# First loads in another order in a Conformer and neighbourhood-attention block, with per-tile normalisation and attention blocks taken in pairs

## What is computed

```python
h = _rmsnorm(x, norm_g)                       # x * rsqrt(mean(x*x) + 1e-6) * norm_g
proj = h @ w_in                               # 1024 x 9216
a_val, a_glu, z_a, q, k, v, z_b, g_logits = split(proj)
y_a = (_conv_module(a_val, a_glu, ...) * silu(z_a)) @ w_pw_a      # 31 taps per channel
attn = _neighbourhood_attention(q, k, v, rpb)                     # 16 heads of 64
y_b = (attn * silu(z_b)) @ w_o_b
merged = sigmoid(g_a) * y_a + sigmoid(g_b) * y_b
out = _rmsnorm(x + merged @ w_out, final_g)
```

## Time and profile before

| | us |
|---|---|
| median of three runs (lowest, highest) | 1900.12 (1898.42, 1902.84) |
| the profiled execution: its time, its span | 1902.6, 1900.6 |
| PE busy in the span | 1829.4 (96%) |
| DVE busy | 1101.3 (58%) |
| ACT busy | 541.0 (28%) |
| POOL busy | 202.7 (11%) |

### The profile page before, as it was taken

One profiled execution on the slowest core, in us unless ns is written; L12 is line 12 of the kernel. 1 busy time (PEld: TensorE's weight loads), 2 busy tenths in 40 slices (PEclk: granted clock), 3 DMA queues, 4 the chain that ended last, 5 costly groups with the idle time before them and its releaser, 6 DMA issues.

```text
span 1900.6 us, 25315 instructions
## 1 busy us (share of the span) xinstructions
PE 1829.4 (96%) x9164; PEld 1466.7 (77%) x9164; DVE 1101.3 (58%) x1574; ACT 541.0 (28%) x1105; POOL 202.7 (11%) x241
## 2 busy tenths in 40 slices
PE   4999999999999999999999999999999999999997
PEld 3778877877777787787778778778777777887775
DVE  3210396677477478567747747856874666435133
ACT  4311123223223323322322332332344234103121
POOL 0020001011001101101100110110110054000001
PEclk9999999999999999999999999999999999999998
DMA  6061201312312221221231223123116655442223
GB/s 241 34 122 56 80 23 50 104 37 71 92 40 67 73 76 59 78 84 35 78 90 35 73 67 85 51 78 84 34 56 245 231 177 172 155 133 82 85 101 121
DMA packets 161486, 173.50 MB, mean 91 GB/s; under 512 B 11031, under 2 KB 117543, under 8 KB 161228
## 3 DMA queue, kind: packets, MB, share of 16 engines
q1 hardware_dynamic: 135164, 108.45, 19.2%
q10 hardware_dynamic: 22320, 49.56, 6.8%
q0 software_dynamic: 3872, 13.75, 2.9%
HBM read 121.03 MB, written 50.68 MB: 90 GB/s over the span
## 4 chain that ended last, share of the span: by engine, by line
PE 83%; DVE 7%; DMA 5%; ACT 2%; issue 1%; SPq 0%; POOL 0%; ACTq 0%; DVEq 0%
PE pg L1267 62%; PE pg L1283 9%; PE pO L1382 4%; PE pS L1356 3%; PE pT L1366 3%; DVE work L989 1%; DMA qk<-gb_d 1%; DVE work L1170 1%; DMA y_sample<-work 1%; DMA work<-tb_d 1%; DVE xs L927 1%; DVE ws L918 1%; DMA work<-in_b_gate 1%; ACT ws L584 1%; DMA y_prompt<-work 1%
## 5 line engine op out<-in xcount | busy, mean ns | idle before, releaser
L1267 PE MATMUL pg<-xs,ws 128*128 128x512 f32 x5760 | 1371.9, 395 | 6.4 <-DVE work L1187 6.3
L1267 PEld LDWEIGHTS pg<-xs,ws 128*128 128x128 f32 x5760 | 1069.3, 189 | 247.6 <-issue 23.2
L989 DVE SCALAR_TENSOR_TENSOR work<-work 128x1551 f32<-128x1551 f32 x240 | 439.1, 1830 | 3.5
L1283 PE MATMUL pg<-ws,xs 128*128 128x512 f32 x1152 | 273.0, 398 | 13.7 <-DVE ws L918 9.9
L1283 PEld LDWEIGHTS pg<-ws,xs 128*128 128x128 f32 x1152 | 220.6, 193 | 63.2 <-DVE ws L918 13.0
L918 DVE TENSOR_TENSOR ws<-raw,ws 128x1024 fp32r<-128x1024 f32 x96 | 117.1, 1222 | 162.5 <-ACT ws L584 162.1
L1063 DVE CUSTOM_DVE_ANT_0 work<-pS,work 128x384 f32<-128x384 f32 (+1 forms) x192 | 91.2, 510 | 201.6 <-PE pS L1356 201.5
L778 ACT ACTIVATE work<-work,small 128x384 f32<-128x384 f32 (+1 forms) x192 | 109.9, 574 | 289.3 <-DVE small L1063 289.3
L532 POOL TENSOR_TENSOR work<-work 128x384 f32<-128x384 bf16 (+1 forms) x72 | 61.7, 858 | 1091.0 <-DVE small L1063 1079.7
L584 ACT ACTIVATE ws<-raw 128x1024 fp32r<-128x1024 f32 x96 | 100.9, 1054 | 114.2 <-PE pg L1267 83.2
L1073 DVE TENSOR_SCALAR work<-work,small 128x384 f32<-128x384 f32 (+1 forms) x192 | 111.0, 578 | 6.7
(11 more groups left out here) (88 smaller groups left out, 881.0 us busy)
## 6 DMA issues: line engine op xcount, KB each, us to landing
raw<-in_w_in SPq DMA_DIRECT2D x72, 512.0 KB, 4.0
work<-v_d SPq DMA_DIRECT2D x128, 96.0 KB, 2.8
v_d<-work ACTq DMA_DIRECT2D x24, 256.0 KB, 2.0
za_d<-work ACTq DMA_DIRECT2D x24, 256.0 KB, 2.0
ga_d<-work ACTq DMA_DIRECT2D x24, 256.0 KB, 2.0
gb_d<-work ACTq DMA_DIRECT2D x24, 256.0 KB, 2.0
work<-c_d POOLq DMA_DIRECT2D x8, 768.0 KB, 12.8
qk<-gb_d SPq DMA_DIRECT2D x24, 256.0 KB, 4.0
```

The costliest lines, as they stand in the source:

```text
L989: nc.vector.scalar_tensor_tensor(cv[:, 0:CLEN], u[:, k:k + CLEN], cur[:, k:k + 1], cv[:, 0:CLEN], ALU.mult, ALU.add).then_inc(tap_ok, 1)
L1267: last = nc.tensor.matmul(pg[b][:], ws[:, wslot(s), wpart, k * P:(k + 1) * P], xs[:, k, xpart, chunk(n)], start=(k == 0 and wpart == 1), s ...
L1283: last = nc.tensor.matmul(pg[b][:], xs[:, k, xpart, t * P:(t + 1) * P], ws[:, wslot(s0 + k // 2), wpart, chunk(k % 2)], start=(k == 0 and ...
```

## The change

1. **Loads.** SP issues token tile 0, then the norm weight broadcast to all 128 partitions (`ngb`, 128 rows), weight pieces 0 and 1, token tile 1, pieces 2 and 3, tiles 2 to 7, pieces 4 and 5, tiles 8 to 11, the masks, and only then the parameter rows. Pieces 2 and 3 land in buffers of their own (`raw2`), and piece 4 is split into a spare place (`spare`, in the tile qk), so that pieces 0 to 5 wait less for one another. The relative-position load for the second head of unit 0 stands behind the values' load.
2. **Normalisation by tile.** Squares, mean, power, scaling, transposes and evacuation go tile by tile instead of four tiles at a time; the scaling also multiplies by `ngb`. The eight transposes of tile t+1 stand in the middle of group t. The parameter rows are transposed between the first and the second half.
3. **Attention in pairs.** Blocks 2c and 2c+1 go together: values of the pair before, then scores of both blocks, in four banks pS. The transposes are issued one head at a time, in four places half a slot apart, all in one bank pT. One bank pO is left.

```diff
+X_SLOT = 4
...
-    if S_PRO <= s < S_YB:
-        return s % 2
-    return s % 4 if s < S_PRO else (s + 2) % 4
+    if s < S_PRO + 1:
+        return (0, 1, 2, 3, X_SLOT, 0, 1, 2, 3)[s]
+    return s % 2 if s < S_YB else (s + 2) % 4
...
-        pS = [ctx.enter_context(nc.psum_tensor(f"pS{i}", [P, CH], F32)) for i in range(2)]
-        pT = [ctx.enter_context(nc.psum_tensor(f"pT{i}", [P, CH], F32)) for i in range(2)]
-        pO = [ctx.enter_context(nc.psum_tensor(f"pO{i}", [P, CH], F32)) for i in range(2)]
-        pH = [pT[0], pT[1], pO[0], pO[1]]
+        pS = [ctx.enter_context(nc.psum_tensor(f"pS{i}", [P, CH], F32)) for i in range(4)]
+        pT = ctx.enter_context(nc.psum_tensor("pT", [P, CH], F32))
+        pO = ctx.enter_context(nc.psum_tensor("pO", [P, CH], F32))
+        pH = [pT, pO, pS[2], pS[3]]
...
+        def pair_at(i, slot):
+            c, r = divmod(slot - 1, 2 * spacing(i))
+            return c if r == 0 and 0 <= c <= BLOCKS // 2 else None
+        def transposed_at(i, slot, half):
+            m = 4 * spacing(i)
+            c, r = divmod(2 * slot + half - 2, m)
+            t = r - (6 if spacing(i) == 3 else 4)
+            if 0 <= t < 4 and 0 <= c < BLOCKS // 2:
+                return 2 * c + t // 2, t % 2
+            return None
...
             load_x(0)
-            sp.dma_start(prow[0:TAPS, :], dw_w[0]).then_inc(par_in, 16)
-            for r, src in ((I_DWB, dw_b[0:1, :]), (I_LNG, ln_g[0:1, :]), (I_LNB, ln_b[0:1, :]),
...
+            sp.dma_start(ngb, norm_g[0:1, :].to_broadcast([P, D])).then_inc(ng_in, 16)
             for s in range(2):
                 piece_s(s, w_rows(w0, C_V * P, s))
             load_x(1)
             for s in range(2, 4):
                 piece_s(s, w_rows(w0, C_V * P, s))
-            sp.wait_ge(ht_ps, KT)
-            load_x(2)
+            for t in range(2, 8):
+                load_x(t)
+            for s in range(4, 6):
+                piece_s(s, w_rows(w0, C_V * P + CH, s - 4))
+            for t in range(8, NT):
+                load_x(t)
+            sp.wait_ge(w_lo, 4)
             sp.dma_start(msk32, masks).then_inc(mask_in, 16)
-            for s in range(4, 8):
+            for r, n, src in ((0, TAPS, dw_w[0]), (I_DWB, 1, dw_b[0:1, :]), (I_LNG, 1, ln_g[0:1, :]),
...
+                sp.dma_start(prow[r:r + n, :], src).then_inc(par_in, 16)
+            for s in range(6, 8):
                 piece_s(s, w_rows(w0, C_V * P + CH, s - 4))
...
+            def normalise(t):
+                if t == 0:
+                    dve.wait_ge(ng_in, 16)
+                dve.wait_ge(rstd_ok, t + 1)
+                x = xt[:, t % 8, :]
+                nc.vector.scalar_tensor_tensor(x, x, rstd[:, t:t + 1], ngb, ALU.mult, ALU.mult).then_inc(xn_ok, 1)
...
+                    if k == 4 and midway is not None:
+                        h_t(midway)
...
+            h_t(0)
+            for t in range(NT):
+                token_group(t, 0, t, 0, True, t + 1 if t + 1 < NT else None)
+            params()
...
+                    c = pair_at(i, slot)
+                    if c is not None and c >= 1:
+                        values(2 * c - 2)
+                        values(2 * c - 1)
+                    if c is not None and c < BLOCKS // 2:
+                        scores(2 * c)
+                        scores(2 * c + 1)
```

More of the change, by code:

```diff
@@ L211, in build, with wt, raw_of @@
               (et0, idle_ws[:, 2 * TOK:2 * TOK + EROWS * ECOLS].bitcast(F32))]
+        spare = qk[:].rearrange("p h t -> p (h t)")[:, 0:2 * D].rearrange("p (h d) -> p h d", h=2)
+        def wt(s, part):
+            return spare[:, part, :] if wslot(s) == X_SLOT else ws[:, wslot(s), part, :]
+        def raw_of(s):
+            return raw2[:, s - 2, :] if s in (2, 3) else raw[:, s % 2, :]
         def home(k):
@@ L255, in build @@
         w_ld = [sem(f"w_ld{i}") for i in range(2)]
+        w_ld2 = [sem(f"w_ld2{i}") for i in range(2)]
+        ng_in = sem("ng_in")
         w_hi, w_lo = sem("w_hi"), sem("w_lo")
@@ L339, in buf, with late_pair_at @@
             return 2 * (b % 2) + h
[L341 to L349, removed]
+        def pair_at(i, slot):
+            c, r = divmod(slot - 1, 2 * spacing(i))
+            return c if r == 0 and 0 <= c <= BLOCKS // 2 else None
+        def late_pair_at(i, slot):
+            return pair_at(i, slot - 1) if slot >= 2 else None
+        def transposed_at(i, slot, half):
[5 more added lines that the diff above has]
+            return None
         def after(eng, sm, count):
@@ L792, in unit @@
                         evac(gi - 1)
-                    b = scores_at(i, slot)
-                    if b is not None and b < BLOCKS:
-                        probs(b, 0)
-                        probs(b, 1)
-                    b = probs_at(i, slot)
-                    if b is not None:
-                        probs_t(b, 0)
-                        probs_t(b, 1)
+                    c = pair_at(i, slot)
+                    if c is not None and c < BLOCKS // 2:
+                        for b in (2 * c, 2 * c + 1):
+                            for h in range(2):
+                                probs(b, h)
+                    for half in range(2):
+                        bh = transposed_at(i, slot, half)
+                        if bh is not None:
+                            probs_t(*bh)
                     if hf == 1 and gi >= 1 and tiles[(gi - 1) // NCH] in (T_ZA, T_GA, T_GB, T_GA2, T_GB2):
@@ L1109, in unit @@
                         evac(gi - 1)
-                    b = scores_at(i, slot)
-                    if b is not None and b < BLOCKS:
+                    c = pair_at(i, slot)
+                    if c is not None and c >= 2 and c % 2 == 0:
+                        take_o(c // 2 - 1)
+                    if c is not None and c < BLOCKS // 2:
+                        for b in (2 * c, 2 * c + 1):
+                            for h in range(2):
+                                scores(b, h)
                         for h in range(2):
-                            scores(b, h)
+                            probs(2 * c, h)
+                    c = late_pair_at(i, slot)
+                    if c is not None and c < BLOCKS // 2:
                         for h in range(2):
-                            probs(b, h)
-                    if b is not None and b >= 4 and b % 4 == 0:
-                        take_o(b // 4 - 1)
+                            probs(2 * c + 1, h)
                     if n == 1 and hf == 0 and not (last and pos == 5):
@@ L1270, in half_group, with token_group @@
                 return last
-            def token_group(g, s0, t, phase, first):
+            def token_group(g, s0, t, phase, first, midway=None):
                 b = g % 2
@@ L1376, in values @@
                     if j == 0:
[L1378 removed]
+                        after(pe, o_out, NCH * i + s)
                     for c in range(nc_):
```

262 lines of the change are left out of this document (133 added, 129 removed).

## The result

Four executions of each kernel side by side: before 1900.47 us (1898.42 to 1902.84), changed **1843.3 us** (1841.66 to 1844.34), a ratio of 0.9698 with the interval 0.9681 to 0.9715. Predicted were 1843.7 us and a range of 1832 to 1870. The profiled execution took 1843.83 us, its span is 1842.0; the span of before is 1900.6, so 58.6 us have gone; the table says where.

A forecast was written before the change was run, and what follows sets the result against it. PE, 96% busy, was taken as the bound, losing time only to late starts, lower clock and interruptions. Start 31.9 plus pairs 24.5 gave 56.4 us off 1900.1: 1843.7 us, range 1832 to 1870.

The forecast's parts named there:

- The start: Stage V up to the units: new load order and normalisation by tile save 31.9 us, bounds 22 and 35.
- the chain of tile 0: Start of stage V: square, mean, power, scaling, transposes and evacuation of the first tile put first mains at 11.0 us.
- Group 0: First group of stage V: ends at 19.8 at full clock, up to 24 at half clock; 21 was taken.
- The parameter transposes: Between the halves of stage V: 8 small transposes, formerly hidden in the start, cost 0.8 us more.
- Pieces 4 and 5 are there early: Second half of stage V: with these loaded early, the stall is 0.6 us instead of 7.1; bounds 0 and 7.1.
- The pairs: Attention: 0.5 us for each of 45 pairs plus 2 us in unit 0 gives 24.5 us, bounds 14 and 42.
- T: Attention: cost of one transposing interruption of the mains, between -0.09 and 0.10 us, taken at 0.03.
- The fixed cost: Attention: interruptions of the mains by values, scores and transposes cost each block 0.61 us beyond pure work.
- A: Attention: fixed cost is each block's own, not that of leaving the mains; pairs give nothing, 1875 us; chance 0.12.
- B: Stage V: piece 0 lands 7 us later than its bytes say, second half's stall stays 7; 1858 us; chance 0.13.
- C: Attention: each second head waits for ACT's copy from the single transposing bank, 96 places; 1940 at 1 us; chance 0.03.
- D: Stage V: the new order does not act, tile by tile no quicker, clock falls more often; about 1898 us; chance 0.02.

The follow-up runs named there:

- rows_early: Changed kernel with the six narrow parameter transfers back ahead of weight pieces 0 and 1; 1849.83 us, ratio 0.9740 to the kernel before.
- before_cut: Kernel before with the 31 rows of taps issued as two transfers of 16 and 15 rows; 1892.67 us, ratio 0.9965 to the kernel before.
- tiles_first: Changed kernel with token tiles 0 to 3 loaded ahead of the broadcast and the weight pieces; 1845.42 us, ratio 0.9723 to the kernel before.
- piece4_late: Changed kernel with piece 4 split only behind all tokens, so pieces 6 and 7 are issued late; 1842.77 us, ratio 0.9706 to the kernel before.
- pairs_only: Kernel before with only the change's attention in pairs, its stage V as before; 1871.85 us, ratio 0.9859 to the kernel before.
- values_apart: Changed kernel with the values of a pair's first block one slot earlier in units 1 to 6; 1855.83 us, ratio 0.9782 to the kernel before.
- scores_apart: Changed kernel with the scores of a pair's second block one slot later in units 1 to 6; 1857.74 us, ratio 0.9782 to the kernel before.
- heads_split: Kernel before with the second head's transposes 6 mains behind the first's in units 1 to 6; 1903.18 us, ratio 1.0024 to the kernel before.

## Why the prediction was right, and where its reasons were not

**The start, 31.9 predicted, 32.7 measured.** The order of the transfers gave the arrival times nearly to the half microsecond: piece 0 used at 8.12 (7.6 for its landing), first mains at 11.18 (11.0), groups 6.35 apart as forecast. In the chain of tile 0 two terms were a little off: the power on one column took 0.55 us, for which the prediction stood on the 1.02 of four columns, and the scaling took 1.28 instead of 1.2. The scaling was done at 8.1 instead of 8.4, yet the mains were not earlier, since DVE split piece 0 from 9.21 on and came to tile 0's low part only at 10.35: here two small errors cancelled. Group 0 ended near 19.8 instead of the 21 chosen between the two clocks. It was the lower clock that came true, for the first twelve mains, and it cost little, as the prediction argued: DVE had split piece 3 only at 17.1, so at the full clock the group would have ended at about 18.4, an estimate from that time and six mains. The parameter transposes cost 0.6 (0.8).

Part of the 32.7 us now has a price of its own: the narrow rows 7.6 (rows_early against the changed kernel, by first scores at 233.6 and 226.0; in the order of before they cost 5.0, by before_cut), the pieces ahead of tiles 1 to 3 3.7 (tiles_first), the stall of the second half 7. What is left, some 14 us, is put down to the work tile by tile, with no hole in which four tiles are squared and scaled, and no low clock behind one. This last part is by subtraction, from prices taken in two different orders of work; no kernel isolated it.

**One step of the start was right for a wrong reason.** "Pieces 4 and 5 are there early", and so a stall of 0.6 instead of 7.1. The stall did vanish, but piece4_late shows that it all but vanishes with piece 4 late as well (0.9 us of waits). The load was short, 3.9 us instead of 5.8, and it is issued before the table transfers have got going, which is the reading that fits both traces. The prediction allowed "some contention" for it, and its lower bound, the old stall, was therefore tied to the wrong condition.

**The pairs, 24.5 predicted, 25.9 measured** (4.1 + 18.4 + 3.4), or 26.4 with unit 7's own 3.9 for the 3.4 that takes in the scatter behind it. T had been chosen within -0.09 to 0.10 for no stronger reason than the middle, so that 0.03 came out at 0.04 is in part luck; the half microsecond for a pair came out at 0.52 (384 keys) and 0.49 (256). The fixed cost summed from the rows, 0.61 a block, was right as a sum: merging saves 0.52 + 2 x 0.04 = 0.60. Each on its own costs 0.39 and 0.44, 0.83 together, so side by side they are 0.2 cheaper than apart, and merged for two blocks cheaper still. Unit 0 gave 4.1 (3.5) in spite of a new fall of the clock: behind the first scores, 24 mains take 7.19 us and not 5.44.

Windows of the changed kernel and of pairs_only in turn, behind the first scores:

```profile
226.90:234.09 7.19, 7.19 (x26) 5.71 (x25) 7.05 (x16) 2.39 (x9) 1.32 (x2) 0.76 0.00 0
```

```profile
258.30:266.00 7.70, 7.09 (x39) 5.64 (x40) 7.56 (x16) 1.99 (x9) 1.31 (x2) 1.00 0.01 2
```

In pairs_only the clock stays at 1.00, and unit 0 takes 125.1 us all the same: DVE is busy nearly throughout both windows, and PE waits instead of running slowly.

**The rivals.** A, that leaving the mains is free, falls with values_apart and scores_apart: the Trainium skill's sentence in "TensorE: Matmul & The Clock Gate", on what each phase is for, that the drain overlaps the next fill, held within a stream of mains (0.227 us from start to start), and nearly so where transposes stand between (0.04 us), but not where values or scores do (0.39 and 0.44). B, that piece 0 comes late all the same, falls with the start's timeline; rows_early shows how it would have looked, at 1849.8. C, the wait for ACT's copy, hasn't come true in units 1 to 7; in pairs_only one such wait of 0.53 us shows, in unit 0's first part, where DVE bounds anyway. D falls with the windows: in stage V the clock rises from its low start and does not fall again.

## What to carry to other kernels

Read a late load by its shares, not by its bytes: one transfer whose row count has no large divisor up to 16, as 31 has none, delays a share of everything that is queued behind it, and cutting it in two (16 and 15) costs a line. Around a stream of equal matmuls, put foreign ones together at one place: beside their own time each leaving costs 0.4 us (values or scores). And look for a broadcast that stands ahead of something urgent, because a PE wait of some 4 us was paid nearly twice, once as a wait and once at the low clock. Last, when a clock column reads full at the very start, compare the distances of equal instructions before believing it.

## What was not expected of the hardware

- 31 rows of 4 KB held back one share of every load behind them by some 8 us; as 16 and 15 rows they cost 0.6 us (first scores at 226.6 instead of 226.0) and nothing clear of the scatter on the whole.
- Waits of the same length ended differently: the 2.2 us that PE waits before unit 0's first scores are the same in every kernel, and the six us behind them are granted 0.72 in before_cut and in all kernels with the new start, but 1.00 in before, pairs_only and heads_split. A wait of 1.26 us brought none, one of 3.9 brought 0.58 over 7 us. What decides in between stays open.
- Groups of the second half that take piece 4 from the tile qk last 5.50 us (95.05 to 100.55 in the timeline), where 24 mains in ws take 5.44: 0.06 for a group, some 0.8 us in all, not followed up.
